# A hybrid attention layer on one core: the modulation in eight pieces instead of four, its start and all orders rewritten

## The reference

```python
mod = silu(c) @ ada_w + ada_b            # 1024 -> 3 x 1024: shift, scale, gate
h = rmsnorm(x, pre_norm_w) * (1 + scale) + shift
proj = h @ w_in                          # 1024 -> 4 x 512 | 3 x 512 | 512 | 4 | 4
o_moba = softmax attention (8 heads of 64, rope, causal) * silu(mg)
q, k, v = silu(causal conv of 4 taps over the 1536 channels dq, dk, dv)
o_dn = gated delta rule (4 heads of 128, chunks of 64: a triangular inverse,
       then a recurrence over 4 chunks), rmsnorm, * silu(dz)
y = concat(o_moba, o_dn) @ w_out
out = x + gate * rmsnorm(y, post_norm_w)
```

## Time and profile before

| | us |
|---|---|
| median of 3 runs | 208.44 (208.24 to 208.79) |
| profiled execution, its own time | 208.55 |
| its span, first to last instruction | 206.5 |
| busy in it: PE / DVE / ACT / POOL | 186.6 / 127.0 / 105.9 / 96.5 |
| DMA | 38.39 MB, mean 186 GB/s |

### The profile page before, as it was taken

One profiled execution on the slowest core, in us unless ns is written; L12 is line 12 of the kernel. 1 busy time (PEld: TensorE's weight loads), 2 busy tenths in 40 slices (PEclk: granted clock), 3 DMA queues, 4 the chain that ended last, 5 costly groups with the idle time before them and its releaser, 6 DMA issues.

```text
span 206.5 us, 4647 instructions
## 1 busy us (share of the span) xinstructions
PE 186.6 (90%) x1863; PEld 171.6 (83%) x1863; DVE 127.0 (61%) x306; ACT 105.9 (51%) x197; POOL 96.5 (47%) x51
## 2 busy tenths in 40 slices
PE   0079999999999989999999999999999999999980
PEld 0078999999999879999988999898999787788860
DVE  0634977752169988988586852677795135963055
ACT  4735573546476499965650445335251465545230
POOL 2003385687984927978642039701800480045400
PEclk9999999999999999999999999999999999999997
DMA  6999999994760587289247802450890094020022
GB/s 229 347 362 357 386 357 367 369 383 117 253 205 4 159 171 207 76 124 285 62 109 242 299 12 51 159 205 3 301 396 22 16 312 183 18 83 0 3 102 102
DMA packets 27881, 38.39 MB, mean 186 GB/s; under 512 B 2818, under 2 KB 21459, under 8 KB 27860
## 3 DMA queue, kind: packets, MB, share of 16 engines
q1 hardware_dynamic: 27572, 37.05, 55.6%
q10 hardware_dynamic: 288, 1.05, 1.4%
HBM read 37.04 MB, written 1.05 MB: 185 GB/s over the span
## 4 chain that ended last, share of the span: by engine, by line
PE 80%; DVE 10%; DMA 3%; SPq 2%; ACT 1%; issue 1%; POOL 1%; DVEq 0%; POOLq 0%
PE bank L1243 18%; PE bank L1245 16%; PE bank L1244 16%; DVE cv L886 6%; PE bank L1444 3%; DMA ada<-in_ada_w 3%; PE bank L1455 3%; PE bank L1432 2%; PE bank L1273 2%; PE bank L1266 2%; PE bank L1550 2%; PE bank L1526 2%; PE bank L1492 1%; SPq L322 1%; PE bank L1557 1%; PE bank L1503 1%
## 5 line engine op out<-in xcount | busy, mean ns | idle before, releaser
L442 POOL TENSOR_TENSOR wlo<-raw,whi 128x1024 fp32r<-128x1024 f32 (+1 forms) x30 | 69.6, 2338 | 75.7 <-ACT whi L520 75.7
L1243 PE MATMUL bank<-hhi,whi 128*128 128x256 f32 x224 | 66.0, 295 | 0.5 <-DVE hlo L837 0.5
L1244 PE MATMUL bank<-hhi,wlo 128*128 128x256 f32 x224 | 64.5, 288 | 0.0
L1245 PE MATMUL bank<-hlo,whi 128*128 128x256 f32 x224 | 64.5, 288 | 0.0
L1243 PEld LDWEIGHTS bank<-hhi,whi 128*128 128x128 f32 x224 | 44.1, 197 | 1.7 <-DVE hlo L837 0.9
L1244 PEld LDWEIGHTS bank<-hhi,wlo 128*128 128x128 f32 x224 | 44.2, 197 | 0.0
L1245 PEld LDWEIGHTS bank<-hlo,whi 128*128 128x128 f32 x224 | 44.0, 197 | 0.0
L520 ACT ACTIVATE whi<-raw 128x1024 fp32r<-128x1024 f32 (+1 forms) x33 | 32.8, 1026 | 15.7 <-DMA raw<-in_w_in 12.1
L886 DVE SCALAR_TENSOR_TENSOR cv<-bank,convh,cv 128x255 f32<-128x255 f32 (+2 forms) x36 | 17.0, 481 | 6.6 <-ACT cv L566 5.5
L865 DVE SCALAR_TENSOR_TENSOR bank<-ada,sml,bank 128x512 f32<-128x512 f32 x22 | 16.6, 753 | 0.6
L1243 PE MATMUL bank<-whi,ohi 128*128 128x512 f32 x32 | 12.8, 400 | 0.0
(11 more groups left out here) (195 smaller groups left out, 348.8 us busy)
## 6 DMA issues: line engine op xcount, KB each, us to landing
raw<-in_w_in SPq DMA_DIRECT2D x20, 512.0 KB, 8.0
ada<-in_ada_w SPq DMA_DIRECT2D x32, 256.0 KB, 7.8
ada<-in_ada_w SPq DMA_DIRECT2D x4, 1024.0 KB, 12.0
raw<-in_w_out SPq DMA_DIRECT2D x8, 512.0 KB, 4.8
raw<-in_w_in SPq DMA_DIRECT2D x5, 384.0 KB, 7.3
qkvs<-in_w_in SPq DMA_DIRECT2D x4, 384.0 KB, 8.0
cv<-in_w_in SPq DMA_DIRECT2D x4, 384.0 KB, 8.6
xs<-in_x ACTq DMA_DIRECT2D x2, 512.0 KB, 3.9
```

The lines of the kernel that those rows point to most:

```text
L442: pool.tensor_tensor(split_u(wlo, n), raw_u(n), split_u(whi, n).bitcast(F32), ALU.subtract).then_inc(lo_done, 1)
L1243: pe.matmul(out, a[0][ia], b[0][ib], start=start, stop=False, skip_group_check=skip)
L1244: pe.matmul(out, a[1][ia], b[0][ib], start=False, stop=False, skip_group_check=skip)
L1245: return pe.matmul(out, a[0][ia], b[1][ib], start=False, stop=stop, skip_group_check=skip)
```

## The change

- c comes in a row tile of its own, first, then the identity; `c_turn` turns it alone into bank 5; silu(c) is computed from there. The other rows come after the first ada_w piece (`prow_turn`, bank 4).
- The modulation has eight pieces of 128 features: 128 columns of shift and 128 of scale. A piece comes in four DMAs of 256 KB (four feature blocks each), four pieces fit at a time. A row of a DMA is 512 B, before it was 1 KB.
- DVE does blocks 0 to 2 of piece 0, TensorE blocks 3 to 7 (`mod_direct`). `modulate` on DVE is gone: ScalarE makes scale and shift columns from the sums in `modulated(q)`, with `scale1` = (1 + scale bias) x norm weight made once by DVE.
- x: ScalarE squares and scales one token block each, DVE the other. A small Sqrt is run ahead of the square.
- `busy(b, n)`: n products of ones over 256 columns into bank b, used by nothing: 4 ahead of c_turn, 3 behind it, 2 and 4 ahead of x_turn(3).
- DVE_LO goes from (2, 38, 40) to (3, 7, 11, 13, 26, 42, 43).
- The lists of SP, POOL, ACT, DVE and PE are reordered throughout.

```diff
-        DVE_K = (6, 8, 8, 8)
+        DVE_K = (3, 8, 8, 8, 8, 8, 8, 8)
+        def ada_piece(q):
+            return ada[q % 2][:, :, q // 2 % 2 * 256:q // 2 % 2 * 256 + 256]
...
             def load_ada(q):
-                if q >= 2:
-                    sp.wait_ge(mod_ready, q - 1)
-                for k in range(NK):
-                    src = ada_w[0, k * P:(k + 1) * P, 0:2 * D].rearrange("p (a n) -> p a n", a=2)[:, :, q * 256:(q + 1) * 256]
-                    sp.dma_start(ada[q % 2][:, k, :].rearrange("p (a n) -> p a n", a=2), src).then_inc(ada_loaded[q % 2][k], 16)
+                if q >= 4:
+                    sp.wait_ge(acc_done, q - 3)
+                if q == 4:
+                    sp.wait_ge(direct_done, NK - DVE_K[0])
+                for hf in range(2):
+                    for a in range(2):
+                        src = ada_w[0, 4 * hf * P:(4 * hf + 4) * P, a * D + q * P:a * D + (q + 1) * P]
+                        sp.dma_start(ada_piece(q)[:, 4 * hf:4 * hf + 4, a * P:(a + 1) * P],
+                                     src.rearrange("(k p) n -> p k n", p=P)).then_inc(ada_loaded[q % 4][hf], 16)
...
+            load_c()
             load_ada(0)
+            load_rows()
+            load_unit(0)
+            load_ada(1)
             load_unit(1)
+            load_ada(2)
+            load_unit(2)
+            load_ada(3)
...
+            load_ada(4)
+            load_ada(5)
...
+            load_ada(6)
+            load_unit(10)
+            load_ada(7)
...
             def modulated(q):
-                act.wait_ge(mod_read, q + 1)
-                act.wait_ge(xT_done, q + 1)
-                for k in (2 * q, 2 * q + 1):
...
+                act.activation(mod_a[:, q:q + 1], b[:, 1:2], ACT.Identity, scale=pcol[:, R_PRE + q:R_PRE + q + 1],
+                               bias=scale1[:, q:q + 1]).then_inc(mod_read, 1)
+                act.activation(mod_b[:, q:q + 1], b[:, 0:1], ACT.Identity, bias=pcol[:, R_SHIFT + q:R_SHIFT + q + 1]).then_inc(mod_read, 1)
+                act.wait_ge(mod_read, 2 * q + 2)
+                act.wait_ge(xT_done[q // 2], 1)
+                act.activation(bank[6 + q % 2][:, 0:S], xT[:, q, :], ACT.Identity, scale=mod_a[:, q:q + 1],
+                               bias=mod_b[:, q:q + 1]).then_inc(h_done, 1)
...
             mask_z(2, 0)
             mask_z(2, 1)
+            gate_sums(0, 0, 4)
+            gate_sums(0, 4, 8)
             merge(2, 0)
+            rope(3)
             merge(2, 1)
...
+            def busy(b, n):
+                pe.wait_ge(ones_set, 1)
+                for _ in range(n):
+                    pe.matmul(bank[b][:, 0:256], ones[:, :], ones[:, 0:1].to_broadcast([P, 256]), start=True, stop=True)
...
+            busy(3, 4)
+            c_turn()
+            busy(3, 3)
+            mod_direct(3)
+            prow_turn()
+            mod_direct(4)
+            mod_direct(5)
             mod_direct(6)
+            x_turn(0)
             mod_direct(7)
-            x_turn(0)
             mod(0)
             x_turn(1)
             x_turn(2)
+            busy(5, 2)
+            busy(3, 4)
             x_turn(3)
+            mod(1)
             qkv_products(0)
             qkv_products(1)
-            mod(1)
             qkv_products(2)
+            mod(2)
             qkv_products(3)
+            mod(3)
...
```

More of the change, by code:

```diff
@@ L134, in build @@
             qkvs = sb("qkvs", [P, NQKV, S], into=e)
-            acc = sb("acc", [P, 2, 512], into=e)
+            acc = sb("acc", [P, 2, 256], into=e)
         with ExitStack() as e:
@@ new lines, in _ @@
+            load_unit(13)
+            load_unit(14)
+            load_gates()
+            load_unit(20)
+            load_unit(16)
+            load_unit(17)
+            load_unit(19)
+            load_unit(18)
+            load_constants()
+            load_unit(22)
+            load_gate(0)
+            load_unit(25)
+            load_unit(24)
+            load_unit(21)
+            load_unit(23)
+            load_unit(27)
+            load_unit(28)
+            load_unit(26)
+            load_unit(29)
@@ L690, in _ @@
             modulated(0)
+            hi(1)
+            xT_copy(1)
             h_hi(0)
-            xT_copy(1)
             xT_copy(2)
-            hi(1)
             xT_copy(3)
+            modulated(1)
+            h_hi(1)
             hi(2)
@@ L699, in _ @@
             hi(5)
-            modulated(1)
-            h_hi(1)
+            modulated(2)
+            h_hi(2)
+            modulated(3)
+            h_hi(3)
             hi(6)
@@ L704, in _ @@
             hi(8)
-            modulated(2)
-            h_hi(2)
             hi(9)
+            modulated(4)
+            h_hi(4)
+            modulated(5)
+            h_hi(5)
             hi(10)
@@ L710, in _ @@
             hi(12)
-            modulated(3)
-            h_hi(3)
+            modulated(6)
+            h_hi(6)
             hi(13)
             hi(14)
+            hi(15)
+            modulated(7)
+            h_hi(7)
             ba_hi()
-            hi(15)
             hi(16)
@@ L1144, in _ @@
             conv(3)
+            conv_silu(0)
             gates_in()
-            conv_silu(0)
             conv_silu(1)
@@ L1152, in _ @@
             cum_copy()
+            rope(1)
             sum_squares(0)
             sum_squares(1)
-            rope(1)
             sum_squares(2)
@@ L1285, in qkv_products @@
                 k = n // 2
-                pe.wait_ge(hlo_done, k // 2 + 1)
+                pe.wait_ge(hlo_done, k + 1)
                 if k == 0:
-                    pe.wait_ge(xT_done, 3 if n == 0 else 4)
+                    for b in range(3 * (n % 2), min(4, 3 * (n % 2) + 3)):
+                        pe.wait_ge(xT_done[b], 1)
+                    if n == 1:
+                        pe.wait_ge(pcol_done, 1)
                 pe.wait_ge(*low_part(n))
@@ L1638, in _ @@
             half(0)
+            ba_turn()
             half(1)
-            ba_turn()
             half(2)
             half(3)
+            cum()
             k_turn(0)
             k_turn(1)
-            cum()
             q_turn(0)
```

534 lines of the change are left out of this document (273 added, 261 removed).

## The result

The changed kernel takes 230.65 us (median of 4 runs, 230.17 to 231.91), the kernel before 208.34 in the same comparison (207.76 to 208.79): ratio 1.108, 95% interval 1.103 to 1.114. I had predicted 205.4 us, and faster. The profiled execution has a span of 229.0 us against 206.5.

The account below looks back on a forecast made before the run. TensorE, busy 90% of the span, was taken as the bound, with much to win only before 21 us. 208.55 - 3.3 (head and projection) + 0.3 (new orders) = 205.55, taken as 205.4 us; range 202.9 to 208.7.

Parts of the forecast that it names:

- the term for the stretch after the projection: Everything behind the projection: same instructions in new orders, 0.3 us lost net, bounds -1 and +3.
- rival 5: After the projection: VectorE's rope(3) and gate sums hold the merges for over 3 us; 207.9 to 209.5 us, chance 0.12.
- silu(c) at 6.0: Head: with c and the identity loaded first, silu(c) is ready at about 6.0 us, against 7.6 before.
- x scaled at 9.2 and 9.6: Head: x, shared by two engines, is scaled at 9.2 us on VectorE and 9.6 us on ScalarE.
- Piece 0 at 8 to 8.6: Head: the first ada_w piece, 1 MB instead of 2, is there at about 8 to 8.6 us, against 11.8.
- mod(0) at 11.9 or, at the low clock, 14.2: Head: mod(0) ends on TensorE at 11.9 us at the high clock, 14.2 at the low one.
- First projection product at 17.7: Start of the projection: TensorE's first product comes at 17.7 us at the high clock, against 21.02 before.
- rival 3: Head: the clock falls again from 8 to 13 us, projection starts at about 20; total 206.7 to 207.6 us, chance 0.10.
- 512-byte rows at 295 GB/s: Loading ada_w in the projection stage: 512 B rows move 295 GB/s, against 350 with 1 KB rows.
- rival 4: Projection stage: 512 B packets run below 250 GB/s and DMA ends last; 213 us at 216, about 210 at 235; chance 0.09.
- rival 1: Projection stage: 512 B pieces cost nothing extra, clock up by 10 us, VectorE alone limits; total 203.7 us, chance 0.27.
- Stage end at 57.3, between 56.6 and 58.4: End of the q, k, v projection: 57.3 us, against 60.6 before, so 3.3 us won.

Follow-up runs that it names:

- e4: The changed kernel with every product of ones left out: 229.25 us, 1.081 of the kernel before.
- e3: The changed kernel with ada_w pieces 2 to 7 loaded in pairs with 1 KB rows: 226.97 us, 1.081 of the kernel before.
- e1: The changed kernel's head and projection, with the kernel before's order of every queue behind the projection: 215.78 us, 1.028 of the kernel before.
- g1: The changed kernel with three w_in transfers put forward and GpSimd held until normalise(2) is done: 214.35 us, 1.026 of the kernel before.

## Why the prediction was wrong

**The step that failed** is the term for the stretch after the projection: "The same instructions in new orders ... I take 0.3 us lost net (bounds -1 and +3)". It measured 18.4. I had walked through the inverse alone (rival 5, rope(3) and the gate sums ahead of a merge), and that was not the place: TensorE waits for no merge there for even 1 us. I had not followed SP's new order to the high parts that each transfer releases, and not asked what stands behind these on ScalarE: moving three transfers gave back 10 to 12 us. Nor had I laid GpSimd's instructions beside VectorE's: one collision was worth 3.1 us of TensorE's time by the profiles, and the two repairs together gave back 15.4 of the 18.4. And each gap was priced, if at all, at its length. The clock makes it dearer. The kernel before around its only wait of 0.8 us, then the changed kernel:

```profile
70.00:80.00 10.00, 8.78 (x74) 1.00 0.89 218
```

```profile
70.00:80.00 10.00, 8.33 (x57) 0.83 0.67 244
80.00:90.00 10.00, 8.41 (x60) 0.83 0.93 167
90.00:100.00 10.00, 6.29 (x41) 0.83 0.20 59
...
140.00:150.00 10.00, 10.00 (x180) 0.83 0.62 214
...
170.00:180.00 10.00, 8.10 (x61) 0.66 0.56 211
```

The last three columns are granted clock, DMA share and GB/s. After the gaps of 2.0, 1.6, 3.7, 2.5 and 3.2 us the clock was granted in part at 1.2 GHz, and 256-column products start 0.21 us apart there, as from 96.4 to 99.6 us; after before's single gap of 0.8 us it stayed at 2.4. The length of one gap does not settle it: in the projection the clock stayed high after a gap of 1.2 us at 38.8, and was low from 52 to 55 us, after two gaps of 0.8 close together (50.6 and 52.0). The lower clock accounts for the 6.1 us of longer busy time, half as much again as the 12.4 us of gaps.

**silu(c) at 6.0**: right, 5.72. **x scaled at 9.2 and 9.6**: right, 9.25 and 9.65. **Piece 0 at 8 to 8.6**: its first half was used at 7.68; when the second half came the trace doesn't say, since TensorE took it up only behind the wait that ended at 10.00. **mod(0) at 11.9 or, at the low clock, 14.2**: it ran from 13.50 to about 14.4, the low branch. The rows of parameters came at 10.00, since their issue stood 2 us behind the first piece, and the single-column passes ran from 11 us on at the low level (granted clock 0.50). **First projection product at 17.7**: wrong, 20.33; it is what rival 3 gave (about 20). The later products of ones (16.09 to 19.5) did raise the clock before it, to 1.00 from 18 us on, beside VectorE's sums of the second piece, but e4 without them is no slower. The prediction's own sum for TensorE at the low clock, 14.2 + 1.9 + 4 to 6 + 1, makes 21.1 to 23.1 and not 20 to 21; the products of ones took 3.4 where it has 4 to 6.

**512-byte rows at 295 GB/s**: right, 292 while only such pieces were landing; rival 4 (under 250) wrong, rival 1 (no cost) wrong, since 1 KB rows moved 350 and the measurement decides, and in e3's trace the stage is shorter with longer rows. (Rivals 1 and 3 are also off in their totals: by the prediction's own sum their stage ends give 204.2 to 204.7 and 207.0 to 207.9.) **Stage end at 57.3, between 56.6 and 58.4**: 64.80. The start took 2.6 us of that, the clock at 52 to 55 us and 4.1 us of idle time the rest. I had found VectorE level with TensorE (4.9 against 4.9 us a piece) and transfers level too, and then took the sum of the terms instead of a margin: where three are level, each one's lateness reaches the end, as e3 suggests.

The range (to 208.7) held the bounds of the parts that I had priced, and gave the new orders of all the queues 3 us.

**Left open**: TensorE's gap of 2.5 us at 137.4 us has no releaser in the profile. It lies inside half(12), between the last two of its products, where the list has no wait. Gaps of this kind (the longest of each run 0.8 to 3.0 us) stand in all ten runs with the changed orders behind the projection, and in none of the seven with before's; they are a cost of the new program that no experiment here takes away. The 2.7 to 5 us that the changed head still costs in e1 and g1 up to ba are not divided between rows, VectorE's low parts and scatter, and the 2.7 to 3.1 us that these two take longer behind ba than the kernel before are not explained. The exchange of VectorE and GpSimd was shown at normalise(2) and at the gate sums, not at each of the other longer instructions.

## What to carry to other kernels

When a change reorders queues, follow each moved transfer to the first instruction that needs it, and name what is ready and stands behind that instruction; a transfer that nothing urgent waited for held a whole engine here (5.7 and 5.2 us). Lay the instructions of VectorE and GpSimd that work in SBUF beside each other, since a step of 0.3 us took up to 2.4 here. A gap of TensorE can cost its length and then the lower clock (here 12.4 and 6.1 us), so one wait of 1.5 us on an engine with slack was the cheapest edit of all.

## What I had not expected of the hardware

- VectorE's step over 4 values took 1.38 us in place of 0.17, four 128 and 256-wide scalings 7.2 in place of 1.0, and four 512-wide sums 11.3 in place of 3.1, beside running instructions of GpSimd. VectorE's sums into PSUM with one operand from SBUF kept their 0.49 us.
- Fourteen products of ones from 1 to 10.4 us halved the 16 single-column products behind them (1.92 against 3.54 us), and the clock was back at the low level for the first projection products at 18.55 (0.21 us apart).
- SP's issues of 256 KB with 512-byte rows took 0.5 us each at the start (4 in 2.11 us) and up to 1.2 later (8 in 9.31). It is not the rows alone: an issue of 384 KB with 3 KB rows took 2.16 us at 9.40, and before's with 1 KB rows 0.5 (8 in 4.19) to 0.9 (8 in 7.18).
